# Convolution's first chunk projected first, its taps spread over VectorE's early waits; biases split on 128 partitions; mean, variance and embedding matmuls reordered

## What is computed

```
proj = rmsnorm(x) @ w_in                      # 1024 -> 3072, six groups of 512: q, f, i, g, u_a, u_b
f = lb + (1 - lb) * sigmoid(fz)               # gated linear recurrence (HGRN2), 4 heads, state carried
o = rmsnorm_per_head(scan(q, log f, 1 - f, i)) * silu(g)
u = u_a * sigmoid(u_b)                        # 512 channels = 4 chunks of 128
c = depthwise_conv(u, 31 taps) + conv_b       # causal; 30 cached frames ahead of the sample
c = silu(layernorm_over_channels(c))          # mean and variance over all 512 channels
x = x + concat(o, c) @ w_out
x = x + moe(rmsnorm(x))                       # top 4 of 32 experts, 2 biases per expert
x = x + sigmoid(rmsnorm(x) @ w_ple_gate) * (p @ w_ple)     # per-layer embedding
y = rmsnorm(x)
```

## Time and profile before

| | |
|---|---|
| three runs, us | 1169.36, 1169.75, 1170.62; median 1169.75 |
| span of the profiled execution | 1169.5 us (the profile gives no other time for it) |
| PE busy | 1099.8 us, 94% |
| DVE busy | 387.6 us, 33% |
| ACT busy | 242.9 us, 21% |
| POOL busy | 21.3 us, 2% |
| HBM traffic | 368 GB/s over the span |
| chain that ended last | PE 53%, DMA 29%, DVE 2%, ACT 1%, issue 1% |

### The profile page before, as it was taken

One profiled execution on the slowest core, in us unless ns is written; L12 is line 12 of the kernel. 1 busy time (PEld: TensorE's weight loads), 2 busy tenths in 40 slices (PEclk: granted clock), 3 DMA queues, 4 the chain that ended last, 5 costly groups with the idle time before them and its releaser, 6 DMA issues.

```text
span 1169.5 us, 14451 instructions
## 1 busy us (share of the span) xinstructions
PE 1099.8 (94%) x5808; PEld 445.4 (38%) x5808; DVE 387.6 (33%) x850; ACT 242.9 (21%) x394; POOL 21.3 (2%) x16
## 2 busy tenths in 40 slices
PE   6999988999999999999999999999898989898987
PEld 4775545333333333333333332333232323232333
DVE  4789978422121212121303030303030303030334
ACT  3531436201111111112020201020202020202035
POOL 1500000000000000000000000000000000000000
PEclk9999997999999999999999999999999999999999
DMA  9924407799999999999999999999999999999951
GB/s 254 387 72 150 155 20 306 289 411 428 428 427 426 430 430 427 426 430 430 427 429 427 430 429 427 427 429 430 428 428 426 430 429 428 428 428 429 428 229 42
DMA packets 44175, 430.83 MB, mean 368 GB/s; under 512 B 4861, under 2 KB 9045, under 8 KB 19471
## 3 DMA queue, kind: packets, MB, share of 16 engines
q1 hardware_dynamic: 40856, 428.83, 88.3%
q10 hardware_dynamic: 3287, 1.54, 0.6%
HBM read 428.53 MB, written 1.83 MB: 368 GB/s over the span
## 4 chain that ended last, share of the span: by engine, by line
PE 53%; DMA 29%; DVE 2%; ACT 1%; issue 1%; DVEq 0%; ACTq 0%; SPq 0%
PE ps L839 27%; DMA arena<-in_w_gate_up 16%; DMA ring<-in_w_gate_up 10%; PE ps L858 9%; PE ps L767 4%; PE ps L800 4%; PE ps L509 4%; DMA ring<-in_w_down 3%; PE ps L777 2%; PE ps L848 1%; PE ps L769 1%; DVE arena L1744 1%; PE ps L823 1%; ACT arena L1203 0%; PE ps L808 0%
## 5 line engine op out<-in xcount | busy, mean ns | idle before, releaser
L839 PE MATMUL ps<-ring,arena 128*64 128x512 f32 x1280 | 291.4, 598 | 7.5 <-DMA ring<-in_w_gate_up 7.5
L858 PE MATMUL ps<-ring,arena 128*64 128x512 f32 x784 | 177.0, 597 | 19.0 <-DMA ring<-in_w_down 9.3
L839 PE MATMUL ps<-arena 128*64 128x512 f32 x768 | 174.5, 597 | 6.7 <-DMA arena<-in_w_gate_up 6.7
L839 PEld LDWEIGHTS ps<-ring,arena 128*64 128x64 f32 x1280 | 86.3, 136 | 182.0 <-issue 170.8
L1835 DVE TENSOR_TENSOR acc<-ps,acc 128x512 f32<-128x512 f32 x64 | 44.3, 692 | 206.9 <-PE ps L800 206.9
L858 PEld LDWEIGHTS ps<-ring,arena 128*64 128x64 f32 x784 | 53.0, 137 | 125.9 <-issue 90.8
L839 PEld LDWEIGHTS ps<-arena 128*64 128x64 f32 x768 | 51.9, 136 | 105.5 <-issue 92.2
L1725 DVE CAST arena<-cst 96x128 bf16 (+1 forms) x17 | 3.8, 222 | 264.2 <-PE ps L839 264.2
L1203 ACT COPY arena<-ps 128x512 f32<-128x512 f32 x32 | 18.8, 586 | 327.4 <-PE ps L848 327.4
L1744 DVE TENSOR_TENSOR arena<-ps,par 128x256 f32<-128x256 f32 x68 | 25.6, 418 | 123.3 <-PE ps L839 118.4
L499 PE MATMUL ps<-arena,ring 128*128 128x288 f32 x256 | 64.2, 409 | 1.1 <-DVE arena L1338 1.1
(11 more groups left out here) (290 smaller groups left out, 836.3 us busy)
## 6 DMA issues: line engine op xcount, KB each, us to landing
ring<-in_w_gate_up SPq DMA_DIRECT2D x80, 2048.0 KB, 35.9
ring<-in_w_down SPq DMA_DIRECT2D x49, 2048.0 KB, 38.3
arena<-in_w_gate_up SPq DMA_DIRECT2D x48, 2048.0 KB, 35.3
arena<-in_w_down SPq DMA_DIRECT2D x15, 2048.0 KB, 39.0
ring<-in_w_in SPq DMA_DIRECT2D x5, 2048.0 KB, 21.5
ring<-in_w_out SPq DMA_DIRECT2D x2, 2048.0 KB, 17.4
arena<-in_w_ple_gate SPq DMA_DIRECT2D x2, 2048.0 KB, 38.5
ring<-in_w_in SPq DMA_DIRECT2D x2, 1024.0 KB, 11.1
```

What stands on the lines that cost most here:

```text
L839: t = mm(ps[h * 64:h * 64 + 64, G + 2 * e + g, :], xT[:, 2 * kk + c, e * 64:e * 64 + 64], w[:, c, lo:lo + 512], start=False, stop=(kk == 3 ...
L858: t = mm(ps[n * 64:n * 64 + 64, PP + e, :], hidT[:, c, half * 64:half * 64 + 64], w[:, c, n * 512:(n + 1) * 512], start=(half == 0 and c = ...
```

## The change

- **Loads.** Two heads, columns 0 to 127 of u_b and of u_a (rows of 512 B), are loaded first in place of the first half of f; then f whole, the biases, q, and the rest of u_b and u_a.
- **PE order.** Chunk 0 of u_b and of u_a is projected ahead of f; the four cached-frame transposes have a function and a place of their own (`turn_cache`).
- **DVE order.** `product(0)` and 24 taps of chunk 0 stand between the four operations on f, two more beside the logarithm, two ahead of the wait for q, three after level 0; later lists of taps are shorter, and the remainder after `outputs_gain(2)` is 8 taps, of 27 before.
- **ACT order.** The gates' sigmoids stand between pairs of exponentials; three `conv_gate` calls remain there, of four.
- **Biases.** The raw biases lie on 128 partitions (quarters of 512 columns); GpSimd does five operations on 512 columns, and 12 DMAs of SP, which wait for it in SP's queue, spread the three parts to `biasb`. `state` waits for these DMAs where it first writes their source.
- **Mean and variance.** The mean's matmuls stand after the first half of `out_first(1)`, the variance's after the second, `out_first(2)` and two embedding pieces behind them. Embedding pieces 1 and 3 move from there to behind the router.

```
@@ SP
-            w_in(0, 0, W // 2, S["w_in_head"])
+            w_in(UB_UNIT, 0, P, S["ub_head"])
+            w_in(UA_UNIT, 0, P, S["ua_head"])
...
-            w_in(0, W // 2, W, full[0])
-            for r in range(3):
-                sp.dma_start(braw[r * E:(r + 1) * E, :], a["b_gate_up"][0]).then_inc(S["raw_in"], 16)
-            for u in range(1, 6):
-                w_in(u, 0, W, full[u])
+            w_in(F_UNIT, 0, W, full[F_UNIT])
+            for q in range(4):
+                sp.dma_start(braw[q * E:(q + 1) * E, :], a["b_gate_up"][0, :, q * W:(q + 1) * W]
+                             ).then_inc(S["raw_in"], 16)
+            w_in(Q_UNIT, 0, W, full[Q_UNIT])
+            w_in(UB_UNIT, P, W, full[UB_UNIT])
+            w_in(UA_UNIT, P, W, full[UA_UNIT])
+            for u in (4, 5):
+                w_in(u, 0, W, full[u])
+            sp.wait_ge(S["bias_split"], 1)
             for r in range(3):
+                for q in range(4):
+                    sp.dma_start(biasb[r * E:(r + 1) * E, q * W:(q + 1) * W],
+                                 bpiece[q * E:(q + 1) * E, r * W:(r + 1) * W]).then_inc(S["bias_in"], 16)
@@ PE
-            columns(0, [0])
+            columns(UB_UNIT, [0])
             turn_params()
-            columns(0, [1, 2, 3])
+            columns(UA_UNIT, [0])
+            turn_cache()
+            columns(F_UNIT)
             turn_frames()
-            columns(1)
-            pe.wait_ge(S["pt_ready"], 1)
-            columns(2, [0])
-            columns(3, [0])
+            columns(Q_UNIT)
+            pe.wait_ge(S["pt_ready"], 2)
+            columns(UB_UNIT, [1])
             level(0)
...
             out_first(0)
             turn_outputs(2)
-            out_first(1)
-            out_first(2)
+            out_first(1, [0])
             pe.wait_ge(S["tail_ready"], 2)
-            pe.wait_ge(full[2], 32)
             for cc in range(H):
                 pe.wait_ge(S["conv_ready"], cc + 1)
                 t = mm(ps[:, 3, 0:T], ones, cacc[:, cc, 0:T], start=(cc == 0), stop=(cc == H - 1))
-                if cc == 1:
-                    per_layer(0)
             t.then_inc(S["mean_mm"], 1)
-            pe.wait_ge(S["pl_ready"], 1)
-            per_layer(2)
+            out_first(1, [1])
...
             t.then_inc(S["var_mm"], 1)
-            pe.wait_ge(S["pl_ready"], 2)
-            per_layer(1)
-            pe.wait_ge(S["csqrt"], 1)
-            per_layer(3)
+            out_first(2)
+            pe.wait_ge(full[2], 32)
+            per_layer(0)
+            pe.wait_ge(S["pl_ready"], 1)
+            per_layer(2)
...
             router(1)
             router(2)
+            per_layer(1)
+            per_layer(3)
             per_layer(4)
             pe.wait_ge(S["msk_ready"], 1)
@@ POOL
-            pool.wait_ge(S["raw_in"], 48)
-            for n in range(2):
...
+            pool.wait_ge(S["raw_in"], 64)
+            link(nc.gpsimd.tensor_copy(high, braw))
+            link(nc.gpsimd.tensor_tensor(bres, braw, high, ALU.subtract))
+            link(nc.gpsimd.tensor_copy(middle, bres))
+            link(nc.gpsimd.tensor_tensor(bres, bres, middle, ALU.subtract))
+            nc.gpsimd.tensor_copy(low, bres).then_inc(S["bias_split"], 1)
@@ DVE
+            product(0)
+            dve.wait_ge(S["pt_ready"], 1)
             for cc in range(H):
+                taps(6, 1)
                 dve.wait_ge(S["f_sig"], cc + 1)
...
             V.tensor_scalar(kf, kf, -1.0, 1.0, ALU.mult, ALU.add)
+            taps(2, 1)
             dve.wait_ge(S["lnf_ready"], 1)
...
+            taps(2, 1)
             dve.wait_ge(S["q_ready"], H)
...
-            dve.wait_ge(S["pt_ready"], 1)
-            product(0)
             masked(0)
-            taps(8, 1)
+            taps(3, 1)
+            product(1)
+            taps(2, 2)
...
-            taps(22)
+            taps(21)
```

More of the change, by code:

```diff
@@ L216, in program, with ub_gate @@
         ubs = KdT_flat[:, 0:H * T]
+        def ub_gate(cc):
+            return So[:, 0:T] if cc == 0 else ubs[:, cc * T:(cc + 1) * T]
         xn = blocks(ple[:, :])
@@ L1025, in level @@
                 fn(lev, lev, ACT.Exp).then_inc(S["lev_exp"], 1)
-            def conv_gate(cc):
-                act.wait_ge(S["proj_mm"], 8 + 2 * cc + 1)
-                fn(h4(ubs)[:, cc, :], ps[:, ROUND[(8 + 2 * cc) % 6], 0:T], ACT.Sigmoid).then_inc(S["ubsig_ready"], 1)
             level(1)
             for cc in range(H):
-                act.wait_ge(S["proj_mm"], 4 + cc + 1)
-                copy(h4(qf)[:, cc, :], ps[:, ROUND[(4 + cc) % 6], 0:T]).then_inc(S["q_ready"], 1)
-            for cc in range(H):
-                conv_gate(cc)
-                level(cc + 2)
+                act.wait_ge(S["proj_mm"], column_turn(Q_UNIT, cc) + 1)
+                copy(h4(qf)[:, cc, :], ps[:, column_bank(Q_UNIT, cc), 0:T]).then_inc(S["q_ready"], 1)
+            conv_gate(1)
+            level(2)
+            level(3)
+            conv_gate(2)
+            level(4)
+            level(5)
+            conv_gate(3)
             def values(b):
@@ L1182, in _ @@
                    accum_out=wsum[:, b:b + 1]).then_inc(S["wexp"], 1)
+            per_layer(1)
+            low(2)
+            per_layer(3)
             per_layer(4)
-            low(2)
             def copy_gathered(j):
@@ L1360, in _, with tap, taps, product @@
             link(V.memset(reset[:, 0:H * T:CH], 0.0))
+            taps_done, taps_made = {}, [0] * H
+            def tap(cc, n=1):
+                for _ in range(n):
+                    convolve(V, own, cc, taps_made[cc], U, cacc, par, taps_done, S["conv_ready"])
+                    taps_made[cc] += 1
+            def taps(n, chunks=H):
+                for _ in range(n):
+                    tap(min(range(chunks), key=lambda c: taps_made[c]))
+            def product(cc):
+                bank = column_bank(UA_UNIT, cc)
+                dve.wait_ge(S["ubsig_ready"], cc + 1)
+                dve.wait_ge(S["proj_mm"], column_turn(UA_UNIT, cc) + 1)
+                V.tensor_tensor(U[:, cc, PAD:PAD + SEQ], ps[:, bank, 0:SEQ], ub_gate(cc)[:, 0:SEQ], ALU.mult)
+                V.tensor_tensor(U[:, cc, UP - DEC:UP], ps[:, bank, SEQ:T], ub_gate(cc)[:, SEQ:T], ALU.mult
+                                ).then_inc(S["u_ready"], 1)
+                dve.wait_ge(S["u_ready"], cc + 1)
+            product(0)
+            dve.wait_ge(S["pt_ready"], 1)
             for cc in range(H):
+                taps(6, 1)
                 dve.wait_ge(S["f_sig"], cc + 1)
@@ L1463, in _ @@
             masked(1)
-            product(1)
-            taps(2, 2)
+            taps(3, 2)
             level_q(3)
@@ L1468, in _ @@
             masked(2)
-            taps(2, 2)
+            product(2)
+            taps(2, 3)
             level_q(4)
@@ L1472, in _ @@
             masked(3)
-            product(2)
-            taps(9, 3)
+            taps(3, 3)
             level_q(5)
@@ L1491, in state @@
                 dve.wait_ge(S["st_ready"], i)
+                if new is St[0]:
+                    dve.wait_ge(S["bias_in"], 16 * 12)
                 for h in range(H):
@@ L1564, in _ @@
             outputs_gain(2)
-            taps(CW * 2 - taps_made[0] - taps_made[1], 2)
             taps(CW * H - sum(taps_made))
```

158 lines of the change are left out of this document (74 added, 84 removed).

## The result

The changed kernel takes 1162.08 us (median of four runs, 1159.84 to 1163.76), the kernel before beside it 1170.18 (1169.36 to 1172.24). The ratio is 0.9927, with a 95% interval of 0.9911 to 0.9943: 8.1 us faster, forecast 1163.2. Three later comparisons of the same kernel gave 0.9944, 0.9930 and 0.9912.

A forecast was written before the change was run, and what follows sets the result against it. The experts' weight stream bounds the kernel, so only time before the first gate-up, where PE and DVE bound in turn, counts. Span 1169.5 - 6.1 - 0.8 + 0.4 = 1163.0, time 1163.2 us; range 1159.8 to 1167.2.

The forecast's parts named there:

- The bound: Experts' weight stream from the first gate-up (211.07 us) to the end: only shifts, so each microsecond saved earlier counts fully.
- Part 1: Early projections, chunk 0 of u_b and u_a first: PE cost 0, apart from 0.4 us waiting for f's load.
- The wait for f: PE before f's matmuls, near 24.7 us: waits 0 to 0.8 us for f's weights, taken as 0.4.
- f's landing: Load of f's weights at the start: another 1 MB costs 2.7 to 4.1 us, so f lands between 24.1 and 25.5.
- Part 2: Bias split on GpSimd and its 12 small DMAs: nothing waits for it, 0 us; DVE only gets more room.
- Part 3: Mean and variance, from 146.51 us to the output projection's second half: restart at 163.2 instead of 169.36, -6.1 us.
- Part 4: Embedding pieces 1 and 3 behind the router: PE 2.6 us late, ranks and gathering save 0.9 and 2.5, net -0.8.
- rival (a): Behind the router: clock does not fall, or rises at the first piece; -3.4 there, 1160.6 us in all; chance 0.17.
- The clock rule: Router stretch: transposes do not count as PE activity like matmuls, so the clock falls again; -0.8 stands, not -3.4.
- Span and time: Whole kernel: the median of the runs lies 0.25 us above the span, turning 1163.0 into 1163.2.

The follow-up runs named there:

- second and third executions: Changed kernel, nothing edited, profiled in two later comparisons; restart of the output projection to first gate-up took 38.56 and 38.62 us.
- first execution: Changed kernel, nothing edited, as profiled beside its main measurement; span 1161.4 us, time 1163.26 us.

## Why the prediction came out as it did

The time was right within 1.1 us, and by the forecast's mechanism. That it was so near is partly luck: the marks moved by 1.6 us more than forecast, and the step from span to time was as much too small (last point).

- **The bound.** Right: 958.4 and 958.5 us from first gate-up to end, and 957.3 to 958.8 in the profiles of all experiments.
- **Part 1**, the projections: 0 forecast, 0.3 measured, whose place stays open (131.31 us from the first projection's start to block 1 of the output projection, 130.97 before); the projections began 0.37 earlier, which makes up for it. The wait for f, +0.4, was 0. The mis-sized term is f's landing, 24.1 to 25.5 forecast and 21.7 measured: 3 MB in front of PE's f landed when 2 MB had before (21.4), so the further 1 MB cost 0.3 us, not 2.7 to 4.1. The Trainium skill's rule ("DMA: Bandwidth & Descriptors", section "Bandwidth"), that DMAs be 1 MiB or more, had made the wait 1.3. This trace shows no such price: both heads, issued from 3.0 on, had landed by 11.7, within 0.1 us of the one load of 1 MB before (2.98 + 8.7).
- **Part 2**, the biases: 0, as forecast, by the marks of the run with them alone. What the forecast called more room on DVE is large there (2.69 us to 0.75 for one operation), and its share in making the early taps possible is untested.
- **Part 3**: -6.1 forecast, -6.7 measured (169.36 to 162.65), all of it behind 146.5, where both kernels stand at the same mark. The mis-sized term is the time from the mean to the sample's piece: PE was free of the variance at 157.4, not 158.1, because mean and variance step on in 1.94 and 2.03 us, where 2.21 was taken for each, and a half of block 1 in 3.43, not 3.57. The last tap was at 150.85 (forecast 150.9).
- **Part 4**: -0.8 forecast, -1.5 measured (restart to first gate-up 40.23 instead of 41.71), and -3.1 in the second and third executions, near the -3.4 of rival (a), although the clock did fall there, for a shorter time. In the first execution its three terms: PE 2.07 late for the ranks (193.90 less the 191.83 at which the choice was there; forecast 2.6), the ranks' matmuls -0.94 (-0.9), the gathering -2.71 (-2.5). The clock came back at 191.0, inside the three pieces as estimated, but 4.6 us into them, not 5.5.
- **The addition of the parts** hid something. The prediction gave part 3 all of -6.1 and part 4 only -0.8; the run with the pieces back shows that their place carries at least 4.5 us in the changed kernel. 2.96 of that lie ahead of the restart, where part 3's sum had already left pieces 1 and 3 out of the path; in the kernel before the same move takes nothing off that stretch. So the -0.8 was the last step of a sum in this order, and not the price of that edit.
- **The clock rule.** The Trainium skill ("TensorE: Matmul & The Clock Gate", section "Part 4: PE-mode transpose"), by which transposes do not count as PE activity in the way of matmuls, spoke for the fall. The trace agrees for this kernel: in all four of its executions the clock fell between 183 and 184.5, after transposes and 32-column matmuls, with PE busy. It does not say when: with piece 3 behind the ranks, and with the taps or the mean late, the same transposes and router matmuls ran at 1.00 (2.59 us for 32). So rival (a) can come about, and its chance of 0.17 had only one execution of the kernel before to go by.
- **Span and time.** The prediction added 0.25 us to the span, from a span and a median that need not be of the same execution. In every run with both on record the time is 1.8 to 2.0 us above the span (1163.26 and 1161.4 here). That error of 1.6 and the parts' of 1.6 (1163.0 of span forecast, 1161.4 measured) cancel, which no reasoning foresaw; the median lies 1.1 below because other executions were shorter than the profiled one.

Which of the three moves matters is now plain. Undone alone in the changed kernel, the early taps cost the whole gain and more (1172.62), the mean's place nearly all (1169.82), the pieces' place more than half (1167.26); the changed kernel took 1160.79 on that chip. Each needs the others: the taps free the mean (else PE waits 8.45 us for it), the mean's place fills PE's wait (else 4.92 us), and the pieces must leave it once it is full (else 2.96 us later). That the taps alone, put into the kernel before, would do nothing is argued from this and was not run.

## What to carry to other kernels

Where PE and DVE take turns as the bound, work moved into the waits of one pays only if the other's queue is reordered to ask for it earlier; price such edits together, and test them by undoing one, not by doing one. Work that lies in a wait is free only while the wait lasts: look at it again after each gain. A wait of about 5 us or more on PE was paid twice here, once as time and once as 1.4 to 2.8 us of low clock behind it. And profile the same kernel more than once before a difference of 1 or 2 us in a stretch is put down to an edit.

## What the runs showed of the hardware

- After an idle time of 4.92 us the same 32 matmuls took 16.76 and 15.40 us; after 0, 0.56 or 1.48 us they took 14.00.
- The clock also falls with PE busy all the time, in transposes and 32-column matmuls (184.2); in the profiles of three kernels with the same matmuls there it does not.
- VectorE and GpSimd slow each other: one operation of 128x1152 elements took 2.69 us beside GpSimd's work and 0.75 without it, and a cast of 32x1024 on GpSimd took 3.19 us beside DVE's running sum and 1.03 earlier, while DVE was mostly idle (spans on GpSimd are rough).
- Executions of one and the same kernel differ by 4 us or more, along with their mean clock. Where it is 0.996 to 0.999 the changed kernel took 1158.19 to 1161.15 us, where it is 0.994 1162.15 to 1165.66, in all 22 executions. Two profiles show where: the changed kernel in the first comparison has the clock at 0.50 in the window of 136.5 above and from 184.2 to 191.0, the second execution, 3.4 us shorter in span, has neither the first stretch nor the second half of the other.

```profile
136.50:137.00 0.50, 0.36 (x4) 0.07 (x1) 0.47 (x2) 0.50 (x5) 0.00 (x0) 1.00 1.22 524
188.00:188.50 0.50, 0.50 (x3) 0.26 (x2) 0.50 (x7) 0.48 (x2) 0.00 (x0) 1.00 1.07 459
```

That is as much as several of the terms above, and sets what a comparison can tell apart. Why the low clock of a stretch comes in one execution and not in another stays open.
